# Down-projection weights of the experts requested by GpSimd instead of SyncE

## The reference

```python
def moe_ffn(h, w_router, router_bias, w_gate, w_up, w_down, ws_gate, ws_up, ws_down):
    ...                       # scores; 8 of 64 experts for each of the 256 tokens, with weights
    def expert_block(args):
        e, tok, wr = args
        xb = h[tok]
        y = (jax.nn.silu(xb @ w_gate[e]) * (xb @ w_up[e])) @ w_down[e]
        return y * wr[:, None].astype(h.dtype)
    ys = lax.map(expert_block, ...)
    routed = jax.ops.segment_sum(ys.reshape(R, D), row_tok, num_segments=N)
    shared = (jax.nn.silu(h @ ws_gate) * (h @ ws_up)) @ ws_down
    return routed + shared
```

## Time and profile before

| | |
|---|---|
| median of the runs | 2304.04 us (2302.16 to 2306.48) |
| the profiled execution | 2306.21 us, with a span of 2304.50 us in the trace |
| PE busy | 2233.5 us, 97% of the span |
| DVE, ACT, POOL busy | 51%, 30%, 1% |
| HBM read | 632 MB, 275 GB/s over the span |
| expert loop | from 1334 us to about 2280 us |
| requests in the loop | 128 of `wgu` and 64 of `wd`, 2048 KB each |

### The profile page before, as it was taken

The page is one execution under the profiler, slowest core; times in us unless marked ns, Lnnn a source line. Parts: engine busy times, 40 slices in busy tenths (PEclk is TensorE's granted clock), DMA queues, the critical chain, the costliest instruction groups (busy, mean ns, idle before and its releaser), DMA issues.

```text
span 2304.5 us, 32866 instructions
## 1 busy us (share of the span) xinstructions
PE 2233.5 (97%) x12818; PEld 1622.8 (70%) x12818; DVE 1173.9 (51%) x1434; ACT 685.9 (30%) x739; POOL 12.9 (1%) x28
## 2 busy tenths in 40 slices
PE   7999999999999999999999899999999999999995
PEld 7999999999988888888887854444444444444442
DVE  5347666666665555455556744444444444444446
ACT  4333333434344433333334311111111111111111
POOL 0000000000000000000000000000000000000000
PEclk9899999999999999999999899999999999999998
DMA  6444444444445555555666479999999999999994
GB/s 259 141 166 142 160 143 147 156 147 148 148 164 190 201 182 200 183 200 183 236 225 240 152 300 426 429 429 428 428 428 428 429 429 429 428 428 429 429 429 188
DMA packets 61451, 635.28 MB, mean 276 GB/s; under 512 B 7344, under 2 KB 7472, under 8 KB 9152
## 3 DMA queue, kind: packets, MB, share of 16 engines
q1 hardware_dynamic: 59472, 627.30, 68.6%
q0 software_dynamic: 752, 4.75, 0.6%
q10 hardware_dynamic: 1152, 2.10, 0.3%
HBM read 632.02 MB, written 2.10 MB: 275 GB/s over the span
## 4 chain that ended last, share of the span: by engine, by line
PE 79%; DMA 13%; DVE 5%; ACT 2%; issue 1%; DVEq 0%; SPq 0%; ACTq 0%
PE bank L273 25%; PE bank L255 19%; PE bank L801 14%; DMA wgu<-wgu 12%; PE bank L835 6%; PE bank L770 4%; PE bank L780 3%; PE bank L483 3%; DVE wlo L1112 1%; PE bank L705 1%; DMA raw<-units 1%; ACT whi L863 1%; DVE cv L1220 1%; PE bank L692 1%; PE bank L750 0%
## 5 line engine op out<-in xcount | busy, mean ns | idle before, releaser
L1112 DVE TENSOR_TENSOR wlo<-raw,whi 128x2048 fp32r<-128x2048 f32 x187 | 428.5, 2292 | 407.1 <-ACT whi L863 405.0
L863 ACT ACTIVATE whi<-raw 128x2048 fp32r<-128x2048 f32 x187 | 357.7, 1913 | 439.0 <-PE bank L273 320.0
L801 PE MATMUL bank<-wgu,xg 128*64 128x512 f32 x2048 | 447.4, 593 | 4.0 <-DMA wgu<-wgu 2.8
L801 PEld LDWEIGHTS bank<-wgu,xg 128*64 128x64 f32 x2048 | 146.1, 137 | 299.2 <-issue 285.8
L255 PE MATMUL bank<-xhi,whi 128*128 128x256 f32 x896 | 260.6, 291 | 3.9 <-DVE wlo L1112 3.9
L255 PE MATMUL bank<-xhi,wlo 128*128 128x256 f32 x896 | 253.4, 283 | 0.0
L255 PE MATMUL bank<-xlo,whi 128*128 128x256 f32 x896 | 253.4, 283 | 0.0
L835 PE MATMUL bank<-wd,eactT 128*64 128x512 f32 x1024 | 226.8, 595 | 0.0
L1619 DVE SCALAR_TENSOR_TENSOR eact<-eth,bank 128x256 f32<-128x256 f32 x32 | 13.5, 422 | 370.8 <-ACT eth L1085 370.8
L273 PE MATMUL bank<-whi,xhi 128*128 128x512 f32 x512 | 199.8, 390 | 0.0
L273 PE MATMUL bank<-whi,xlo 128*128 128x512 f32 x512 | 199.2, 389 | 0.0
(11 more groups left out here) (331 smaller groups left out, 3420.6 us busy)
## 6 DMA issues: line engine op xcount, KB each, us to landing
wgu<-wgu SPq DMA_DIRECT2D x128, 2048.0 KB, 20.6
raw<-units SPq DMA_DIRECT2D x210, 1024.0 KB, 4.8
wd<-wd SPq DMA_DIRECT2D x64, 2048.0 KB, 16.7
h<-xtok POOLq DMA_DIRECT2D x2, 1024.0 KB, 8.6
out<-acc SPq DMA_DIRECT2D x4, 512.0 KB, 2.7
poolmix<-poolm ACTq DMA_DIRECT2D x4, 256.0 KB, 4.5
poolwt<-poolw ACTq DMA_DIRECT2D x4, 256.0 KB, 4.6
ln_gain<-lnp POOLq DMA_DIRECT2D x1, 1024.0 KB, 7.5
```

The lines of the kernel that those rows point to most:

```text
L801: mi = nc.tensor.matmul(bank[3][CAP * j:CAP * j + CAP, :], buf[:, 4 * c + k, CAP * (2 * half + j):CAP * (2 * half + j + 1)], wgu_t[c][:, j ...
L863: nc.scalar.activation(whi[u % SPLIT][:, :], raw[u % RAW][:, :], ACT.Copy).then_inc(hi_done, 1)
L1112: V.tensor_tensor(wlo[u % SPLIT][:, :], raw[u % RAW][:, :], whi[u % SPLIT][:, :].bitcast(f32), ALU.subtract).then_inc(lo_done, 1)
```

## The change

GpSimd requests d0 and d1 of all pairs, with the same waits on the same semaphores, and SP requests only g0 to g3. GpSimd's part stands behind its last request of before. For pair 0 it waits for the same count of `unit_used` behind which SP had d0. The loads of further rounds stay with SP, but they do not run here.

```diff
         def load_down(pair, it):
             for c in range(2):
-                if it is not None:
-                    sp.wait_ge(ex["d_free"] if c == 0 else ex["y_ps"], (it if c == 0 else it * 4) + START)
-                elif c == 1:
-                    sp.wait_ge(sh["dps"], 8)
+                sp.wait_ge(ex["d_free"] if c == 0 else ex["y_ps"], (it if c == 0 else it * 4) + START)
                 sp.dma_start(wd_t[c][:, :, :], wd[pair, c]).then_inc(d_full[c], 16)
 
-        def load_pair(it, pair):
+        def load_gate_up(it, pair):
 
             for c in range(4):
                 sp.wait_ge(ex["gu_free"], it * 4 + (c - 3) + START)
                 sp.dma_start(wgu_t[c][:, :, :, :], wgu[pair, c]).then_inc(gu_full[c], 16)
-            load_down(pair, it)
...
-        load_down(0, None)
         sp.wait_ge(rt["rounds_ok"], 1)
         with sp.Fori(1, PAIRS) as pair:
-            load_pair(pair, pair)
+            load_gate_up(pair, pair)
...
         pool.dma_start(lnb[0][:, :], lnp[1].partition_broadcast(P)).then_inc(og["ln_in"], 16)
+
+        pool.wait_ge(unit_used, N_D0 - N_X)
+        pool.dma_start(wd_t[0][:, :, :], wd[0, 0]).then_inc(d_full[0], 16)
+        pool.wait_ge(sh["dps"], 8)
+        pool.dma_start(wd_t[1][:, :, :], wd[0, 1]).then_inc(d_full[1], 16)
+        with pool.Fori(1, PAIRS) as pair:
+            pool.wait_ge(ex["d_free"], pair + START)
+            pool.dma_start(wd_t[0][:, :, :], wd[pair, 0]).then_inc(d_full[0], 16)
+            pool.wait_ge(ex["y_ps"], pair * 4 + START)
+            pool.dma_start(wd_t[1][:, :, :], wd[pair, 1]).then_inc(d_full[1], 16)
```

More of the change, by code:

```diff
@@ L351, in _ @@
                 with sp.Fori(0, PAIRS) as pair:
-                    load_pair(b * PAIRS + pair, pair)
+                    load_gate_up(b * PAIRS + pair, pair)
+                    load_down(pair, b * PAIRS + pair)
         sp.wait_ge(ex["gu_free"], n_rounds * (4 * PAIRS) + START)
```

## The result

The changed kernel takes 2309.62 us (median of 20 runs), the one before 2304.8 us (20 runs). The ratio is 1.0025, with a 95% interval of 1.0018 to 1.0031: 5.8 us more, between 4.1 and 7.1. (The two medians alone lie 4.8 us apart.) Forecast were 2310.7 us and 6.65 us more.

A forecast was written before the change was run, and what follows sets the result against it. PE bounds the loop early, transfers late (29.37 us a pair against 28.88). Zero for moved requests plus L = (11.1 + 2.2) / 2 = 6.65 us puts the median of 2304.04 at 2310.7 us; range 2306 to 2317, own range 2307.5 to 2313.

The forecast's parts named there:

- What bounds the kernel: Expert loop: PE sets the pace early, transfers from pair 21 on, with 5.3 us of PE waits for g3.
- SP's requests gain nothing, GpSimd's cost nothing by themselves: Expert loop: removing 64 requests from SP gains 0; adding the same 64 to GpSimd costs 0.
- Order of service: Loop's DMA queues: at half the rate each, d0 and d1 overtake older g bytes; g3 lands later, 6.65 us including a.
- Start of a GpSimd transfer, a = 2.2 us: At d0 of pair 1: a GpSimd transfer starts 2.2 us later than SP's, and all loop bytes finish that much later.
- L for the last pair alone: L, PE's lateness against before, was worked out at pair 31 as (11.1 + a) / 2 = 6.65 us, same for every pair.
- The sum: Whole kernel: span and execution each 6.65 us longer, so the median becomes 2310.7 us.
- A: Loop's DMA queues: unequal shares following packet lengths; 2312.2 us with two thirds to GpSimd, 2309 to 2315 with one third; chance 0.22.
- B: Loop's DMA queues: engines serve the oldest request first, so only a is left; 2306.2 us; chance 0.12.
- C: Loop's transfers: two queues fill small gaps, 436 GB/s needed, and 5.3 us of waits go; 2298.7 us; chance 0.06.
- D: GpSimd's loop requests held up by DVE copies; 4.4 us free, 2337 us at 5.5; chance 0.08 with other rate losses.

The follow-up runs named there:

- half_sp: Kernel before, but SP loads only half of each down load of pairs 1 to 31; ratio to before 0.9982, loop 895.6 us.
- all_gpsimd: Kernel before, but GpSimd requests all six loads of each pair in SP's old order, one queue; ratio to before 0.9999, loop 901.6 us.
- down_act: Changed kernel, but ACT requests the down loads of pairs 1 to 31 and SP those of pair 0; ratio to before 1.0021, loop 906.5 us.
- d0_gpsimd: Changed kernel, but GpSimd requests only d0; d1 stays in SP's queue behind g3; ratio to before 1.0026, loop 905.9 us.
- d1_gpsimd: Changed kernel, but GpSimd requests only d1; d0 stays in SP's queue behind g3; ratio to before 1.0011, loop 904.5 us.
- swapped: Changed kernel with requesters exchanged: GpSimd requests all gate and up loads, SP all down loads; ratio to before 1.0030, loop 905.9 us.
- last1_gpsimd: Kernel before, but GpSimd requests the down loads of pair 31 only; ratio to before 1.0053, loop 913.1 us.
- split_g: Changed kernel, but SP requests each gate and up load in two pieces with 8 KB rows; ratio to before 1.0061, loop 917.3 us.
- half_gpsimd: Changed kernel, but GpSimd loads only half of each down load of pairs 1 to 31; ratio to before 0.9978, loop 895.5 us.
- split_d: Changed kernel, but GpSimd requests each down load in two pieces with 8 KB rows; ratio to before 1.0040, loop 912.4 us.

## Why the prediction was right, point by point

**What bounds the kernel.** Bytes from pair 21 on, 5.3 us of waits: right. half_sp takes them away and is 5.2 us shorter in the loop.

**SP's requests gain nothing, GpSimd's cost nothing by themselves.** Right; all_gpsimd is within 0.1% of before, and both half kernels have one loop time.

**Order of service.** The step on which all hung, and right: equal shares at equal packets, g3 late, PE waits on `wgu` ahead of pair 17 (from pair 10), 10.3 us of waits in the loop where 12 were forecast. Four variants have the loop time that this count gives within 0.5 us (down_act, d0_gpsimd, d1_gpsimd, swapped), and in last1_gpsimd g3 lands as late as worked out, though its loop is 3 us longer than that. d0_gpsimd and last1_gpsimd are the two that no cost of requests can give. The rule of the Trainium skill (DMA: Bandwidth & Descriptors, Queues, rings and completion order) that an engine changes queues at packets fits these runs also where the forecast's rows had nothing to show, at 8 KB against 16 KB: two thirds to one third. They show equal numbers of packets, not how many an engine takes at a turn.

**Start of a GpSimd transfer, a = 2.2 us.** This term was mis-sized. The row of `h` did not have nothing ahead of it: SP's 1 MB, requested at 1109.8, landed only at 1114.6, 3.5 us after `h` was requested. d0 of pair 1 shows 7.9 us against 7.6, so 0.3; the 0.4 us of the Trainium skill (DMA: Bandwidth & Descriptors, Specifications) was nearer. With 0.3 the same formula gives 5.7 us, and the loop has 5.1.

**Start beside a full queue.** This term the forecast did not have. With a = 0.3 and half the rate d0 would land after 3.0 + 9.8 = 12.8 us, and it takes 14.0; in split_g it takes 11.5 and not 10.4; in swapped, where SP requests d0, 13.6 and not 12.5. In the changed kernel the stretch from the request of d0 of pair 30 to 2217 us, 3.25 us, has packets of SP's queue alone:

```profile
q1 hardware_dynamic: 104, 1.47, 106.6%
```

So overtaking begins some 1.2 us later than counted, while the g bytes go on. My estimate from these landings, made afterwards: 9.9 - L of g are left then, g3 lands at 2245.0 + L + 2 x (9.9 - L) = 2254.6 + L, and L = 5.1 us. In that count the bytes as a whole are 0.3 us late. The trace has 0.7: counted from the start of gate and up of pair 1, the last down load lands at 892.3 us and not at 891.7. With 0.7, L = 5.5 us. In the forecast a was 1.9 us too long, which is 0.95 of its 6.65, and this start takes off 0.6 more; 5.1 are left. No run isolates the term, and for d1_gpsimd it would give 3.1 us where 3.8 were measured.

**L for the last pair alone.** The formula takes one lateness for all pairs. In fact PE waits 1.0 us in every second pair, pair 31 has no wait, and what counts is the lateness that pair 30 leaves. The estimates above leave this out as well, so that their nearness to the 5.1 us measured is in part luck.

**The sum.** 6.65 us forecast, 5.8 measured over 20 runs, and 5.1 in the loop of the one profile. The 1.7 us behind the loop in this profile come from the clock. They are in the profiles of half_gpsimd and split_g too (10.9 us there, 9.2 in half_sp), and 1.0 of them in those of last1_gpsimd and split_d, but not in those of down_act, d0_gpsimd or swapped; whether they belong to the 5.8 of the median stays open.

**The rivals.** A does not apply, since both queues' packets have 16 KB here, but its mechanism is real: split_d and split_g show it. B (oldest first) and C (more than 428 GB/s together) are refuted by the landings and by 428 GB/s in the loop of the changed kernel, swapped and down_act. D (requests held up by DVE): in half_gpsimd GpSimd's loads land 0.3 us later than SP's in half_sp, and 4.4 us would have been free, so no.

No variant that loads all the bytes beats the kernel before. By the theory none that only moves requests can, though this is argued and not tried further: d0 and d1 of pair 31 are the bytes that are used last, and SP's single queue serves them last.

## What to carry to other kernels

When the DMA engines have no gap, a second queue adds no bytes (428 GB/s with one and with two); it only changes who is served first. Put on it only what is needed no later than what it overtakes, and ask of each load how long after landing it is used: here, before the change, d had 5 to 7 us to spare and g3 none. No run here that loads all the bytes beats the one queue in the order of use, and the lateness it avoids is paid once, at the end, for the last load that is overtaken.

## What the runs showed of the hardware

- Two queues at work share the DMA engines by equal numbers of packets: 51.7% and 49.2% of the time with 16 KB rows on both, 68.7% and 32.8% with 16 against 8 KB (split_d). It does not matter which engine requests (swapped, down_act).
- Cutting loads into halves with rows of 8 KB in place of 16 costs rate in a saturated stretch: 428 GB/s with all rows at 16 KB, 426 with a third of the bytes at 8 KB (split_d), 424 with two thirds (split_g). Whether the rows cost it or the doubled number of requests was not separated.
- A wait can cost more than its length: behind waits of 3.69 and 4.42 us PE's clock was granted at 0.65 in the mean (first line below, last1_gpsimd from 2259 us), where the waits of about 1 us in every second pair of the changed kernel left it at 1.00.
- The clock ahead of the loop differs between the profiles. The first gather takes 8.20 us in the trace of the changed kernel, above, and 10.77 in that of all_gpsimd, second line below, with the same instructions of PE; the clock was granted at 1.00 in the one and at 0.71 in the other (third and fourth line). Gate and up of pair 1 began between 1367.2 and 1372.8 us in the thirteen profiles of the kernels here, which is why spans of single profiles don't tell 5 us. There is one profile of each kernel, so whether this goes with the kernel or with the execution is not shown.

```profile
2259.00:2266.00 7.00, 6.66 (x23) 2.46 (x24) 0.30 (x1) 0.38 (x1) 0.00 (x0) 0.65 0.01 2
```

```profile
1329.29 10.77 PE bank L776 x64
```

```profile
1331.00:1339.00 8.00, 7.96 (x64) 7.87 (x64) 2.08 (x3) 2.39 (x4) 0.00 (x0) 1.00 0.52 220
1329.00:1340.00 11.00, 10.71 (x64) 10.49 (x64) 2.23 (x4) 2.39 (x4) 0.00 (x0) 0.71 0.39 163
```
